# FFN up projections of a two-block transformer kernel as seven block products in place of eight, all weight splits and sums on GpSimd

## What is computed

```python
h = rms_norm(x, norm_ffn_pre[l])
u = causal_dwconv(h @ ffn_w_up[l], ffn_conv_w[l]) + ffn_conv_b[l]    # width 3, over tokens
gate, up = jnp.split(u, 2, axis=-1)                                  # 2 x 2816 features
x = x + rms_norm((jax.nn.silu(gate) * up) @ ffn_w_down[l], norm_ffn_post[l])
```

## Time and profile before

| | |
|---|---|
| median of three runs | 2310.47 us (2310.32 to 2311.59) |
| span of the profiled execution, first to last instruction | 2307.0 us |
| start and end around that span, against the median | 3.5 us |
| TensorE busy | 2228.0 us, 97% |
| VectorE busy | 1170.0 us, 51% |
| GpSimd busy | 1019.7 us, 44% |
| ScalarE busy | 716.6 us, 31% |
| mean granted TensorE clock | 0.993 |

### The profile page before, as it was taken

The page is one execution under the profiler, slowest core; times in us unless marked ns, Lnnn a source line. Parts: engine busy times, 40 slices in busy tenths (PEclk is TensorE's granted clock), DMA queues, the critical chain, the costliest instruction groups (busy, mean ns, idle before and its releaser), DMA issues.

```text
span 2307.0 us, 27430 instructions
## 1 busy us (share of the span) xinstructions
PE 2228.0 (97%) x9862; PEld 1728.0 (75%) x9862; DVE 1170.0 (51%) x1240; ACT 716.6 (31%) x1132; POOL 1019.7 (44%) x821
## 2 busy tenths in 40 slices
PE   7999999999899999999999988999999999999998
PEld 5777755577688888888887766777767777788887
DVE  6864355546654433333333878666665556411223
ACT  4243256633311111111112344555344334200112
POOL 3533410176644444444444663232235653444475
PEclk9999999999999999999999999999999999999999
DMA  5111100132211111111111231000101111111153
GB/s 205 50 37 37 37 10 10 38 127 73 66 53 45 53 47 45 52 48 45 46 54 46 76 131 44 28 27 27 37 28 37 54 36 37 46 51 49 45 164 119
DMA packets 34031, 130.61 MB, mean 57 GB/s; under 512 B 4132, under 2 KB 4516, under 8 KB 33196
## 3 DMA queue, kind: packets, MB, share of 16 engines
q1 hardware_dynamic: 30960, 111.39, 15.1%
q10 hardware_dynamic: 3004, 18.30, 2.1%
HBM read 117.04 MB, written 12.58 MB: 56 GB/s over the span
## 4 chain that ended last, share of the span: by engine, by line
PE 84%; DVE 4%; ACT 4%; issue 4%; POOL 2%; DMA 1%; SPq 0%; ACTq 0%; POOLq 0%; DVEq 0%
PE PG L671 14%; PE PG L677 13%; PE PG L676 13%; PE PG L1219 5%; PE PG L1225 5%; PE PG L1224 5%; PE PG L1026 2%; PE PO L1290 1%; PE PO L1048 1%; PE PT L1040 1%; PE PG L730 1%; DMA WR<-weights 1%; PE PG L736 1%; PE PG L735 1%; POOL WH L564 1%
## 5 line engine op out<-in xcount | busy, mean ns | idle before, releaser
L564 POOL TENSOR_TENSOR WH<-WR,zero 128x512 fp32r<-128x512 f32 x380 | 417.2, 1098 | 1182.4 <-PE PG L671 666.9
L567 POOL TENSOR_TENSOR WL<-WR,WH 128x512 fp32r<-128x512 f32 x380 | 541.0, 1424 | 29.8
L671 PE MATMUL PG<-HH,WH 128*128 128x512 f32 x1136 | 450.0, 396 | 2.0 <-POOL WL L567 1.2
L677 PE MATMUL PG<-HH,WL 128*128 128x512 f32 x1136 | 443.4, 390 | 0.0
L676 PE MATMUL PG<-HL,WH 128*128 128x512 f32 x1136 | 443.2, 390 | 0.0
L671 PEld LDWEIGHTS PG<-HH,WH 128*128 128x128 f32 x1136 | 213.8, 188 | 51.1 <-issue 4.5
L676 PEld LDWEIGHTS PG<-HL,WH 128*128 128x128 f32 x1136 | 213.7, 188 | 46.1 <-issue 2.4
L677 PEld LDWEIGHTS PG<-HH,WL 128*128 128x128 f32 x1136 | 213.8, 188 | 44.9
L1219 PE MATMUL PG<-HH,WH 128*128 128x512 f32 x544 | 226.0, 415 | 5.6 <-ACTq L2074 2.7
L1225 PE MATMUL PG<-HH,WL 128*128 128x512 f32 x544 | 213.1, 392 | 0.0
L1224 PE MATMUL PG<-HL,WH 128*128 128x512 f32 x544 | 212.3, 390 | 0.0
(11 more groups left out here) (542 smaller groups left out, 4134.2 us busy)
## 6 DMA issues: line engine op xcount, KB each, us to landing
WR<-weights SPq DMA_DIRECT2D x196, 512.0 KB, 3.5
RAW<-x SPq DMA_DIRECT2D x8, 512.0 KB, 7.7
x_spill<-X ACTq DMA_DIRECT2D x1, 4096.0 KB, 12.6
X<-x_spill ACTq DMA_DIRECT2D x1, 4096.0 KB, 13.0
x_spill<-X ACTq DMA_DIRECT2D x4, 1024.0 KB, 5.4
X<-x_spill ACTq DMA_DIRECT2D x8, 512.0 KB, 4.0
y<-RAW SPq DMA_DIRECT2D x7, 512.0 KB, 5.0
POSI<-positions ACTq DMA_DIRECT2D x1, 512.0 KB, 15.2
```

The source lines that it names most:

```text
L564: pool.tensor_tensor(WH[:, slot, part], WR[:, slot, part], zero[:, :].to_broadcast([P, HALF]), ALU.add).then_inc(w_hi, 1)
L567: pool.tensor_tensor(WL[:, slot, part], WR[:, slot, part], WH[:, slot, part].bitcast(F32), ALU.subtract).then_inc(w_split, 1)
L671: m = pe.matmul(out[:, cut], WH[:, slot, w], hi[:, cut], start=n == 0, stop=False)
L677: m = pe.matmul(out[:, cut], WL[:, slot, w], hi[:, cut], start=False, stop=last)
```

## The change

**Seven products in place of eight.** For one tile, gate and up (2 blocks of output), upper and lower half of the contraction (2), and left and right half of the tokens (2) make a 2x2 by 2x2 block product: 8 block products of 12 matmuls. The change makes it with 7 (Strassen's scheme in Winograd's form): `block_products` runs 84 matmuls in place of 96 on sums and differences of weight blocks and of input blocks. Tiles 3 to 21 are made so; tiles 0, 1 and 2 as before.

**Weights.** `low` splits a part as before (L690, L692). `block_sums` also makes four sums or differences of weight parts in `WR` (L714), each 128x512. A tile has 7 parts to split instead of 4, and 4 sums. SP loads by counts of split parts `u_lo`. Each tile still has two units of weights.

**Inputs.** The four extra input forms are made once, from the normed input that is now kept in place in `X`: `form_sum` and `form_low` on DVE, `form_high` on ACT, four of each, 128x2048, beside tiles 1 and 2 and the first down products. To free `X`, the residual is sent to memory in front of the norm (`put_away`: two transfers of 1 MB, then four of 512 KB) and brought back in two of 2 MB near the end of the FFN.

**Outputs.** The four output blocks have to be put together from four PSUM banks of 512: ACT copies twice (`first_copy`, `second_copy`), DVE adds five times 128x512 (`add`, L3100), into `CG` and `CU` in SBUF. ACT's first tap and DVE's other two (`tap`, L3105) then read `CG` and `CU` in place of PSUM. The rounding of the gated product moves from ACT to DVE (`split_product`, L3087, a 128x1024 copy).

**Order.** The loop runs nine turns of down products, tile, tile; one tile (`ffn_next`) stands in front of it and one behind it (`tail`). The memset of `RAW` is gone: the first down products are copied.

The core of the diff:

```diff
+            def low(k, hi_done, raw):
+
+                pool.tensor_tensor(part_of(WH, k), raw, zero[:, :].to_broadcast([P, HALF]), ALU.add).then_inc(u_hi, 1)
+                pool.wait_ge(u_hi, hi_done)
+                pool.tensor_tensor(part_of(WL, k), raw, part_of(WH, k).bitcast(F32), ALU.subtract).then_inc(u_lo, 1)
...
+                lows(0)
+                b.loaded(pool, 1)
+                combine(1, upper_1, upper_1, lower_1, ALU.subtract, 1)
+                combine(2, lower_1, lower_1, lower_2, ALU.add, 1)
+                lows(1)
+                combine(3, upper_1, lower_2, upper_1, ALU.subtract, 2)
+                lows(2)
+                lows(3)
+                lows(4)
+                combine(4, upper_2, upper_2, upper_1, ALU.subtract, 5)
+                lows(5)
+                lows(6)
...
+            with sp.Fori(0, TURNS) as i:
+                for n, (done, s) in enumerate(((2, 0), (4, 1), (10, 1), (11, 0), (17, 0), (18, 1))):
+                    sp.wait_ge(u_lo, PARTS * i + done)
+                    load_at(6 * i + (FFN_RAW + 2 + n), s)
...
-            with pe.Fori(0, FFN_PAIRS - 2) as i:
-                g = Groups("ffn", i, 8)
-                gate_up(g, 0, 0, i, 6)
-                down(down_banks(i), 2, i, i, 6)
-                gate_up(g, 6, 4, i, 6)
-            for x in range(2):
-                gate_up(Groups("ffn_tail"), 2 * x, 2 * x, stage="ffn_tail")
+            gate_up(Groups("ffn_next"), 0, 0, stage="ffn_next")
+            with pe.Fori(0, TURNS) as i:
+                down(down_banks(i), i)
...
+                block_products(Blocks(i))
...
+                block_products(Blocks(i, 1))
+            block_products(Blocks(0, tail=True))
```

More of the change, by code:

```diff
@@ new lines, in program, with __init__, raw, loaded @@
+        RAW_PARTS = ((0, 0), (0, 0), (1, 0), (0, 0), (0, 1), (1, 1), (0, 1))
+        SUMS_MADE = {1: 1, 2: 2, 3: 3, 6: 4}
+        class Blocks:
+            def __init__(self, i, second=0, tail=False):
+                self.i, self.second = i, second
+                self.part0 = 4 + 7 * second
+                if tail:
+                    self.i, self.second, self.part0 = TURNS, 0, 0
+            def raw(self, k):
+                unit, q = RAW_PARTS[k]
+                return WR[:, (unit + self.second) % 2, halves(q)]
+            def loaded(self, eng, unit):
+                turn = 1 + self.second if self.part0 else 0
+                eng.wait_ge(w_loaded[(unit + self.second) % 2],
+                            self.i * 48 + 16 * (FFN_RAW // 2 + turn + 1))
+            def banks(self):
+                if self.second:
+                    return [PG[:, n // 2, halves(n)] for n in range(4)]
+                return [PT[:, 0, :], PT[:, 1, :], PO[:, 0, :], PO[:, 1, :]]
+            def part(self, k):
+                return self.i * PARTS + (self.part0 + k + 1)
+            def product(self, k):
+                return self.i * 14 + (7 * self.second + k + 1)
+            def summed(self, n):
+                return self.i * 8 + (4 * self.second + n)
+            def added(self, n):
+                return self.i * (2 * FFN_ADDS) + (FFN_ADDS * self.second + n)
+            def copied(self, n):
+                return self.i * (2 * FFN_COPIES) + (FFN_COPIES * self.second + n)
+            def tile(self, n):
+                return self.i * 2 + (3 + self.second + n)
+            def twice_tile(self, n):
+                return self.i * 4 + (6 + 2 * self.second + n)
+            def taps(self, n):
+                return self.i * 4 + (2 * self.second + n)
+            def vector(self, part, tap):
+                c = VEC0["ffn_conv"] + 8 * (3 + self.second) + 4 * part + tap
+                if isinstance(self.i, int):
+                    return vec[:, c + 16 * self.i:c + 16 * self.i + 1]
+                return vec[:, bass.ds(16 * self.i + c, 1)]
@@ L1919, in last_square @@
+            tail = Blocks(0, tail=True)
+            first_copy(tail)
+            second_copy(tail)
+            for h in range(2):
+                act.dma_start(X[:, :, halves(h)], spill3[:, :, halves(h)]).then_inc(x_away, 16)
+            block_tap(tail, 1)
+            block_tap(tail, 0)
+            block_silu(tail)
             def last_square(n):
@@ L2798, in low, with split_product @@
-            def low(pair, x, hi=GH, lo=GL):
-                tile_no = 2 * pair + x
-                dve.wait_ge(f_hi, tile_no + 1)
+                    g.ready(dve, part)
+                    taps(g, part, buf, [ffn_vec(part, 2 - d, tile_no // 2, tile_no % 2) for d in (1, 2)], None)
+                g.wait_free(dve, 1)
+                product(tile_no + 1)
+            def split_product(done, x, hi=GH, lo=GL):
+                dve.wait_ge(f_prod, done)
+                step(dve.tensor_copy(hi[:, x, :], PRD[:, :]))
@@ L2805, in accumulate @@
+            def accumulate(banks, first=False):
                 for m in range(KT):
```

441 lines of the change are left out of this document (321 added, 120 removed).

## The result

The changed kernel takes **2371.85 us** (median of 4 runs, 2368.09 to 2372.82), the kernel before 2310.72 beside it: a ratio of 1.0265, with a 95% interval of 1.0251 to 1.0279. It is slower by 61 us, as forecast in sign and place, and by 9.9 us more than the forecast. The profiled execution has a span of 2371.0 us, 64.0 above that of before.

The account below looks back on a forecast made before the run. GpSimd was predicted to replace TensorE as the bound, at 69.3 us a turn: 9 x 4.0 - 1.7 + 1 + 15 + 1.5 = +51.8 on a 2307.0 us span, so 2362 us with 3.5 around it; range 2324 to 2392.

Parts of the forecast that it names:

- GpSimd's share: Loop turn: splits 42.6, sums 10.9, loads 4.2, VectorE 11.6 make 69.3 us, 4.0 more than before.
- The rounding copy: Loop: VectorE's rounding copy holds GpSimd up 0.4 us each, two a turn, 0.8; other end 0.
- 0.90 a tap: Loop: each of 12 VectorE operations a turn with two SBUF inputs holds GpSimd up 0.90 us, 10.8 in all.
- rival 2: Loop: GpSimd and TensorE about even at 65 us a turn, tail +10 to 13, kernel 2322 us; chance 9%.
- First turn, -1.7 against the others: First loop turn: less to wait for, GpSimd comes with three parts ready, 1.7 us less.
- In front, +1: Before the loop: norm's wait for `X` to reach memory costs 0, at most 2 us; 1 us added for the forms.
- Tile 21, +7: Tile behind the loop: no down products in front, GpSimd gets no lead, 29 us against 21.8, +7.
- Last downs, +1 and +7: Last downs: first wait 3.4 to 4.0 us in place of 2.67, +1; three parts beside tile 21's VectorE operations, +7.
- +1.5 for the return of `X`: Last downs: weight loads beside the 4 MB return of `X` take 5.0 us, +1.5; other end +8.
- Rival 1: Loop: TensorE stays the bound, 61.5 us a turn, kernel 2283 us; chance 8%.
- Rival 3: Loop: gaps of 3 to 4 us turn TensorE cold; if half a turn, 75 us a turn, 2410; chance 5%.
- Rival 4: Loop: VectorE's chain of bank-freeing adds behind stretched taps is the bound, kernel 2380 us; chance 2%.

Follow-up runs that it names:

- the pair of added operations: Changed kernel plus eight overwritten 128x512 VectorE operations a turn: both inputs in SBUF, 2381.94 us; control with one input in PSUM, 2369.35 us.
- The late return: Changed kernel with the two transfers bringing the residual back issued some 15 us later, behind the last tile's SiLU: 2369.74 us.
- The kernels that do free GpSimd: Changed kernel with weight-block sums cut to two columns (2311.38 us), taps cut to two columns (2316.97), or 14 high parts a turn made by ScalarE (2316.02).
- the operations from PSUM: Changed kernel plus eight VectorE operations a turn, 128x512, one input in PSUM, results overwritten: 2369.35 us.
- ScalarE's kernel: Changed kernel with 14 of a turn's 18 high parts made by ScalarE: 2316.02 us; with its order mended at both loop ends, 2307.56 us.
- the kernel with half loads: Changed kernel with the six weight loads a turn cut from 512 to 256 KB: 2361.00 us.

## Why the prediction was right, and where it was off

- **GpSimd's share, 69.3 us a turn, not 65.28**: right, and 69.83 measured. Its terms held one by one: parts and sums at the rows' lengths, loads 4.1 (4.2), VectorE 12.0 (11.6). That the sum was possible at all rests on the earlier trace rows, a place in another stage where both engines were dense: the taps' 1.0 us could not be read from the FFN of before. The rounding copy was counted at 0.4 with 0 as its other end. It takes 1400 ns now, and 0.69 in the one place where it did not have to wait (1296.60); GpSimd's low part beside it took 1.64 there, in place of 1.29, so 0.35 was its price. That the sum of the VectorE terms came out so near is in part luck: 0.90 a tap was 0.1 too low, and what the taps and the copies leave of the 12.0 is 0.8 for each of the four others, which was 0.1 too high.
- **The Trainium skill's rules.** The trace had shown VectorE and GpSimd lengthening each other, and the pair of added operations shows that it is the second SBUF input that does it: "GPSIMD Engine Reference" of the Trainium skill, key points, says that, and the trace agrees. The count of cycles in its section on elementwise cycle accounting would have led to 2325, rival 2; the rows have 1.29 us for the operation that an estimate from the page puts at 1.11, and led to 2362, which was nearer.
- **First turn, -1.7 against the others**: wrong in sign, +2.4 (72.15 against 69.8). The step took GpSimd's lead into account and not the forms, whose VectorE operations on 2048 columns with two SBUF inputs lie beside GpSimd's first parts. I had priced them for VectorE's time alone ("beside tile 2 and the first down products"), though the same rule stood one paragraph above. GpSimd's operations beside the forms took 3.1 to 3.4 us, and TensorE's first wait for GpSimd in that turn is 4.12 us; one of 2.02 for VectorE, which had the forms in front of its taps, lies before it:

```profile
651.74 3.22 POOL L692 TENSOR_TENSOR WL<-WR,WH 128x512 fp32r<-128x512 f32 x1
...
702.68 0.64 PE L1355 MATMUL PG<-T3H,WH 128*128 128x512 f32 x1 [4.12 <-POOL WL L692]
```

  This is argued from the timeline; no run took the forms out alone.
- **In front, +1**: +4.8 in the trace, of which 3.75 lie before the restart, where kernels with the same code scatter by 4.4. What is left is +1.1, and -0.2 to +0.7 in the nine other traces of the changed kernel and what was made from it. (The 650.1 us that the prediction gives for the first down product is 647.22 in the trace of before; its sum does not use it.) The cause named for its bound, the transfer of `X`, did not show: GpSimd's and VectorE's new reads were suspected and cost nothing that could be measured either.
- **Tile 21, +7**: +7.1.
- **Last downs, +1 and +7, and +1.5 for the return of `X`**: +10.0 in place of 9.5, by two errors against each other. The wait grew by 4.9 and not by 2.5, because the unit that GpSimd waited for landed in 7.7 us and not in 5.0; the end of the range given for it, +8, held it. The parts grew by 5.1 and not by 7: GpSimd's late start moved half of them out from under the taps. The late return shows the exchange.
- **Rival 1**, TensorE stays the bound, would have come out at 61.5 us a turn and 2283. The kernels that do free GpSimd stop at 63.5 to 64.3: this rival's time was too low by 18 to 25 us. **Rival 3**, a cold TensorE, happened about as priced and decided nothing: once a turn, behind a wait of 2.5 to 3.8 us, six to ten matmuls came at the lower level of the clock, about 1.5 us, inside TensorE's slack (granted clock 0.97 over the seven turns, 1.00 before). **Rival 4** is excluded by the operations from PSUM.

So 61 us slower is GpSimd's load against TensorE's: the change takes 5.4 us of work a turn from the engine that was the bound and gives 34 to one that had 36 to spare (GpSimd is busy 444.51 / 7 = 63.5 us a turn now, 29.0 before), and its waits, 6.3 a turn of which 4.1 are for loads, do the rest.

## What to carry to other kernels

Before moving elementwise work to GpSimd, write down its turn with three terms besides its operations: every VectorE instruction with two SBUF inputs (about 1 us each for 1024 columns here), every load that it frees the buffer for, and what it must wait for before it can start. Where GpSimd sets the pace, changing an operand from PSUM to SBUF on VectorE is an edit of GpSimd's time too; where it did not, in front of the FFN, it cost nothing. And price the first and the last turn by themselves: here they held 23 of the 64 us, and the 8.5 us that brought ScalarE's kernel level with the kernel before came from them alone.

## What the runs showed of the hardware that I had not expected

- The lengthening is mutual and not in proportion to length. Added VectorE operations of 512 columns went from 687 to 1305 ns and cost GpSimd 0.25 us each; three of the four forms of tap went to 1.8 to 2.0 us, and the eight taps of a turn cost it 1.0 each. Which of the two engines' operations is lengthened differs from place to place: at 978.28 it is GpSimd's alone, at 957.62 a GpSimd operation keeps its 1.05 us and VectorE's copy beside it takes 1.43.
- ScalarE reading `WR` and writing `WH` in SBUF beside both took 626 ns on average and never more than 636, in 133 operations, of which 75 ran beside a VectorE operation with SBUF inputs. Nor does it lengthen GpSimd's low part: beside ScalarE's high part, and with no such VectorE operation near, that took 1.28 to 1.30 us, as it does alone.
- After the wait of 2.54 us at 986.29 TensorE's matmuls came every 0.43 us six times over, the lower of its two levels, and after one of 1.32 us, in ScalarE's kernel, at once every 0.24:

```profile
1023.58 0.50 PE L1349 MATMUL PG<-XR,WH 128*128 128x512 f32 x1 [1.32 <-POOL WL L700]
1023.92 0.40 PE L1351 MATMUL PG<-XR,WH 128*128 128x512 f32 x1
```

  The length of a wait does not decide this by itself. The wait of 2.63 us at 980.74, in the same turn, was followed by matmuls every 0.23 to 0.24 us, and so was that of 3.41 us in the kernel with half loads.

- Two 512 KB loads issued beside 4 MB of other transfers landed after 7.7 and 9.3 us, in place of 3.5.
